# Stick-breaking attention: the suffix sums as split float32r products instead of plain float32 products

## The chip, the core and the metric

The kernel runs on one core of a Trainium2 chip. The metric is the device time of one execution in microseconds (us). The engines are TensorE (PE, matrix products into PSUM), VectorE (DVE), ScalarE (ACT), GpSimd (POOL) and SyncE (SP, which issues the loads). Each works through its own queue in order; they wait for each other on semaphores.

## The reference, cut to what matters

The program is two models one after the other, 256 tokens wide. The change touches the second model's stick-breaking attention (two layers, eight heads of 64):

```python
z = jnp.einsum('bqhd,bkhd->bhqk', q_blk, k).astype(jnp.float32) * scale
past = kpos[None, :] < qpos[:, None]
log_beta = jax.nn.log_sigmoid(z)
log_one_minus = jnp.where(past, jax.nn.log_sigmoid(-z), 0.0)
remain = lax.cumsum(log_one_minus, axis=3, reverse=True) - log_one_minus
w = jnp.where(past, jnp.exp(log_beta + remain), 0.0)
return jnp.einsum('bhqk,bkhd->bqhd', w.astype(v.dtype), v)
```

With s = softplus(z) = max(z, 0) + ln(1 + exp(-|z|)) one has log_one_minus = -s and log_beta = z - s, so the exponent is z minus the sum of s over all keys from the present one on (below the query). That sum over keys is a product with a triangle of ones inside a block of 128 keys, and with a square of ones for the whole later block.

## The kernel before, in words

Weights come in units of 128x1024 float32. Each is loaded by SyncE into `raw` (4 slots), rounded to float32r by ScalarE (`w_hi`, L941), and the remainder `w_lo` = raw - w_hi is formed by VectorE (L1341). A unit is then 24 products of TensorE (L2592 to L2594: high x high, low x high, high x low, for 8 slices), and ScalarE evicts the result (L1230, L1232). ScalarE and VectorE split unit q + 3 while unit q is being multiplied. TensorE starts unit q when the result of unit q - 2 is evicted and `w_lo` of q is there.

The attention stage of a layer of the second model has 48 such units, and the steps of three attentions are laid between them by ticks, one tick to a unit: `block2_items` puts each step on a tick, `ordered` sorts the steps of a tick by `IN_TICK`, and each engine runs its own part of that one list in order. In a tick the unit comes last. The stick-breaking part handles the eight heads as four pairs; tile shapes are 128 keys x (2 heads x 384), the 384 being 256 queries for the first key block and 128 for the second:

- ticks 12 to 15, `sb_scores`: TensorE makes the scores (L2699), VectorE scales and masks them into `sb_z` (L1956), ScalarE makes `sb_e` = |z| and then exp(-|z|) (L1269, L1271);
- ticks 16 and 17, `sb_log`, two pairs each: ScalarE makes ln(1 + e) (L1276), VectorE adds max(z, 0) (L1962). Now `sb_e` holds s, and `sb_soft` is counted up;
- ticks 19 to 22, `sb_remain`: TensorE makes the sums into `turn2`, two banks of PSUM (L2712 to L2714), VectorE subtracts them from `sb_z` (L1968, counts up `sb_diff`), ScalarE takes exp (L1281). As there is one `turn2`, the products of pair j wait for `sb_diff` of pair j - 1;
- ticks 21 to 24, `sb_values` and `sb_out`: the product with the values (L2725) and the split of its result (L1941, L1943).

Beside them stand, at ticks 17, 20 and 24 (and others), rope steps of two tiles: TensorE L2615, VectorE L1860 and one tick later L1867, GpSimd L2141. These are all that GpSimd does in the stage.

A plain float32 product appears in the trace as two instructions, a float32r product as one.

Of the kernel before, what the change touches and what calls it, by code (L numbers as in the profile page):

```python
# [33 lines left out]
F32 = mybir.dt.float32  # L34
F32R = mybir.dt.float32r
ALU = mybir.AluOpType
ACT = mybir.ActivationFunctionType
AX = mybir.AxisListType
P = 128
D = 1024  # L40
KD = D // P
S = 256
# [82 lines left out]
def build_program(nc, x, c, ctx, c_ctx, w_mod, b_mod, norm_g, ffn_w_in, ffn_w_out, w_in, conv_w, pool_w,  # L125
# [3 lines left out]
    K = 1024  # L129
    base = 17 * K  # L130
    region = {}
    at = base
# [6 lines left out]
    def fixed(name, shape, dt, offset):  # L139
        return nc.alloc_sbuf_tensor_at(name, shape, dt, offset=offset)  # L140

    def small(name, shape, dt=F32):
# [55 lines left out]
    sb_z = fixed("sb_z", [P, 4, 2, 384], F32, region["scr"])  # L198
    sb_e = [fixed(f"sb_e{j}", [P, 2, 384], F32, region["scr"] + 12 * K if j == 3 else region["g"] + (30 + 3 * j) * K)
            for j in range(4)]  # L200
    k_swap = fixed("k_swap", [P, S], F32, region["bias"] + 8 * K)
    rope_t = fixed("rope_t", [P, 2, S], F32, region["bias"] + 9 * K)

    const = small("const", [P, CONSTS.shape[1]])
    ones = small("ones", [P, P])
# [40 lines left out]
    for ap in vec_rows:  # L246
        done = 0
        while done < ap.shape[0]:
            n = min(ap.shape[0] - done, P - r % P)
# [12 lines left out]
    def table(name):  # L262
        a, b = CONST_COLS[name]
        return const[:, a:b]

    ident, rot, tri = table("ident"), table("rot"), table("tri")
# [6 lines left out]
    score2, turn2 = psum[:, 4:6, :], psum[:, 6:8, :]  # L273


    def sem(name):
        return nc.alloc_semaphore(name)
# [88 lines left out]
    sb_scores = sem("sb_scores")  # L366
    sb_remain = sem("sb_remain")
    sb_scaled = sem("sb_scaled")
    sb_soft = sem("sb_soft")
    sb_diff = sem("sb_diff")  # L370
    sb_log = sem("sb_log")
    sb_weight = sem("sb_weight")

    c_ready = sem("c_ready")
    mix_pool = sem("mix_pool")
# [223 lines left out]
    def add_job(at, j, start, weights, turn, values):  # L599
# [4 lines left out]
        if j["what"] != "near" or j["qt"] == 1:  # L604
            at(start + values, "out", j)

    IN_TICK = ("values", "sb_values", "weights", "turn", "scores", "sb_scores", "sb_log", "sb_remain", "out", "sb_out",
               "rope_add", "swap", "rope", "turn_v", "bias", "conv_in", "conv_out", "sigmoid", "unit")

    def ordered(ticks):  # L610

        return [item for tick in sorted(ticks) for item in sorted(ticks[tick], key=lambda item: IN_TICK.index(item[0]))]

# [40 lines left out]
    def block2_items(at_):  # L654
        layer = at_["layer"]
        ticks = {}

        def at(tick, what, arg):
            ticks.setdefault(tick, []).append((what, arg))
        for q in range(at_["fill"].n):  # L660
            at(q, "unit", (q, 0, 1))
        for tick, tiles in ((0, (4,)), (1, (0, 1)), (2, (2, 3)), (17, (18, 19)), (20, (22, 23)), (24, (20, 21)), (26, (24, 25))):
            r = dict(tiles=tiles, r=counts["rope"])
            counts["rope"] += 1
            at(tick, "rope", r)
            at(tick + 1, "rope_add", r)
        at(1, "swap", None)
        for tick, j in ((4, 0), (12, 1), (14, 2), (25, 3), (28, 4)):
            at(tick, "turn_v", j)
        jobs = [new_job("swa", pair, 0, layer) for pair in range(4)]  # L670
        for m, j in enumerate(jobs):
            add_job(at, j, SWA_FIRST + 2 * m, 1, 3, 4)
        sb = []
        for pair in range(4):
            z = dict(pair=pair, n=counts["sb"], first=pair == 0)
            counts["sb"] += 1
            sb.append(z)
            at(12 + pair, "sb_scores", z)
            at(16 + pair // 2, "sb_log", z)
            at(19 + pair, "sb_remain", z)  # L680
            at(21 + pair, "sb_values", z)
            at(21 + pair, "sb_out", z)
        moba = [new_job("moba", pair, 0, layer) for pair in range(4)]
        for m, j in enumerate(moba):
            j["first"] = m == 0
            add_job(at, j, 25 + 4 * m, 2, 3, 4)
        for i, tick in enumerate((42, 44, 48)):
            at(tick, "sigmoid", i)
        at_["jobs"], at_["sb"] = jobs + moba, sb
        return ordered(ticks)  # L690
# [241 lines left out]
    def _(act):  # L932
# [14 lines left out]
        for s, name in enumerate(("c", "c_ctx")):  # L947
            ins = act.activation(c_pad[:, :, s], vec(name, 0, KD), ACT.Silu)
# [324 lines left out]
        def act_sb_log(z):  # L1273
            j = z["pair"]
            act.wait_ge(sb_log, z["log0"] + 8 + j)
            act.activation(sb_e[j][:, :, :], sb_e[j][:, :, :], ACT.Ln, bias=ones[:, 0:1]).then_inc(sb_log, 1)  # L1276

        def act_sb_remain(z):
            z_ = sb_z[:, z["pair"], :, :]
            act.wait_ge(sb_diff, z["n"] + 1)  # L1280
            act.activation(z_, z_, ACT.Exp).then_inc(sb_weight, 1)  # L1281
# [6 lines left out]
        def act_attend(at_):  # L1288
            split, turned = set(), set()
            for what, arg in at_["items"]:  # L1290
                if what == "unit":
                    act_unit(at_, *arg, split=arg[0] not in split)
                elif what == "scores":
                    if arg["what"] == "swa":
                        q = SWA_FIRST + 2 * arg["pair"]
                        split_ahead(at_["fill"], q % 4, q // 4)
                        split.add(q)
                    if arg["what"] == "swa" and arg["pair"] > 0:
                        last = at_["jobs"][arg["pair"] - 1]
                        act_turn(last)  # L1300
                        turned.add(last["n"])
                    act_scores(arg)
                elif what == "turn":
                    if arg["n"] not in turned:
                        act_turn(arg)
                elif what == "sb_scores":
                    act_sb_scores(arg)
                elif what == "sb_log":
                    act_sb_log(arg)
                elif what == "sb_remain":  # L1310
                    act_sb_remain(arg)
                elif what == "conv_in":
                    act_conv(at_["mixed"])
                elif what == "pooled":
                    act_pooled(at_["mixed"])
                elif what == "sigmoid":
                    act_sigmoid(at_, arg)
# [713 lines left out]
    def _(pool):  # L2031
# [105 lines left out]
        def pool_rope(r):  # L2137
            w, t0 = len(r["tiles"]), r["tiles"][0]
            cos = table("cos").unsqueeze(1).to_broadcast([P, w, S])
            pool.wait_ge(rope_pe, r["r"] + 1)  # L2140
            pool.tensor_tensor(U2[:, t0:t0 + w, :], U2[:, t0:t0 + w, :], cos, ALU.mult).then_inc(rope_pool, 1)  # L2141

        def pool_norm(nm):
            kind, width = nm["kind"], nm.get("width", S)
            if kind == "first":
                pool.wait_ge(mod_ready, 1)
                pool_w_load(0)
                bias_load(0)
            elif kind in ("plain", "double"):
                for k in range(KD):  # L2150
                    pool.wait_ge(h_hi_done, nm["h0"] + k + 1)
                    pool.tensor_tensor(H2_lo[:, k, :], T2[:, k, :], H2_hi[:, k, :].bitcast(F32), ALU.subtract).then_inc(h_lo_done, 1)

        for kind, ph in plan:
            if kind == "gemm" and ph.kind != "fill":
                pool_gemm(ph)
            elif kind == "norm":
                pool_norm(ph)
            elif kind == "mixers":
                pool_mixers(ph)  # L2160
            elif kind == "attend":
                if ph["block"] == 1:
                    if ph["layer"] + 1 < DEPTH:
                        pool.wait_ge(max_done, ph["jobs"][-1]["n"] + 1)
                        pool.wait_ge(mix_pe, 4)
                        pool_w_load(ph["layer"] + 1)
                        bias_load(ph["layer"] + 1)
                else:
                    for what, arg in ph["items"]:
                        if what == "rope":  # L2170
                            pool_rope(arg)


    @blk.tensor
    def _(pe):
# [525 lines left out]
            ins.then_inc(sb_scores, 1)  # L2701

        def pe_sb_remain(at_, z):
            pe.wait_ge(sb_soft, z["n"] + 1)
            if z["first"]:
                pe.wait_ge(pt_copy, z["free_scores"])
            else:
                pe.wait_ge(sb_diff, z["n"])
            for e in range(2):

                x_ = sb_e[z["pair"]][:, e, :]
                pe.matmul(turn2[:, e, 0:S], tri, x_[:, 0:S], start=True, stop=False)  # L2712
                pe.matmul(turn2[:, e, P:S], ones[:, :], x_[:, S:384], start=False, stop=True)
                ins = pe.matmul(turn2[:, e, S:384], tri, x_[:, S:384], start=True, stop=True)  # L2714
            ins.then_inc(sb_remain, 1)

        def pe_sb_values(at_, z):
# [75 lines left out]
```

## Time and profile before

| | us |
|---|---|
| median of 3 runs (2587.07 to 2588.83) | 2587.65 |
| span of the profiled execution (its own time as the profile has it) | 2584.8 |
| median less span | 2.85 |
| TensorE busy, share of the span | 2541.3, 98% |
| VectorE busy | 1889.3, 73% |
| ScalarE busy | 1137.2, 44% |
| GpSimd busy | 376.0, 15% |

The profile shows one execution, from its first instruction to its last; no other time is listed for that execution. Busy is the time in which an engine had an instruction under way. Products of TensorE overlap each other, so the cost of one is read from the distance between two starts and not from its duration. On the other engines, too, an instruction begins some 0.1 us before the one ahead of it has ended. In a row of the timeline, "x2" are two instructions drawn together, and brackets at the end give the idle time before them and what ended it; no brackets mean no idle time.

### The profile page before, as it was taken

The page shows a single profiled execution, that of the slowest core. Times are in us where ns is not written, and L with a number is a line of the kernel's source. Part 1 is how long each engine was busy: PE and PEld are TensorE (multiplying, and loading weights), DVE is VectorE, ACT ScalarE, POOL GpSimd, SP SyncE. Part 2 cuts the span into 40 slices and gives each one's busy share as a digit, 9 for nine tenths or more (in the row PEclk, how much of TensorE's full clock was granted, in tenths as well). Part 3 has the DMA queues.
Part 4 walks back from the last instruction along what each step waited for, and adds up shares of the span by engine and source line. Part 5 has one row for each costly group of instructions (what it writes and reads, how often), then busy time and mean ns, then how long its engine had stood idle before and what let it go on. Part 6 is the DMA issues. An engine that isn't in the chain of part 4 may idle for free. (4 is left out here: it accounts for less than half of the span.)

```text
span 2584.8 us, 42675 instructions
## 1 busy us (share of the span) xinstructions
PE 2541.3 (98%) x15774; PEld 2238.7 (87%) x15774; DVE 1889.3 (73%) x2915; ACT 1137.2 (44%) x1791; POOL 376.0 (15%) x359
## 2 busy tenths in 40 slices
PE   7999999999999999999999999999999999999999
PEld 4888889779888888888887888889999998999998
DVE  5899985666868678687465777786578877657886
ACT  3222233444222233222244555655656565565655
POOL 2101011141101021000020200210021121002111
PEclk9999999999999999999999999999999999999999
DMA  9566653134454535554232466544566654456664
GB/s 302 169 196 195 196 171 101 58 85 137 150 174 148 175 110 171 159 166 155 88 104 87 123 190 189 159 139 125 161 181 180 186 173 140 122 163 181 179 183 128
DMA packets 653991, 400.48 MB, mean 155 GB/s; under 512 B 12007, under 2 KB 614724, under 8 KB 653698
## 3 DMA queue, kind: packets, MB, share of 16 engines
q1 hardware_dynamic: 651520, 394.67, 50.2%
q0 software_dynamic: 2048, 3.48, 0.9%
q8 instruction: 109, 1.79, 0.3%
q14 instruction: 56, 0.46, 0.1%
q10 hardware_dynamic: 258, 0.09, 0.0%
HBM read 397.14 MB, written 1.05 MB: 154 GB/s over the span
## 5 line engine op out<-in xcount | busy, mean ns | idle before, releaser
L1341 DVE TENSOR_TENSOR w_lo<-raw,w_hi 128x1024 fp32r<-128x1024 f32 x609 | 762.1, 1251 | 262.2 <-ACT w_hi L941 258.5
L941 ACT ACTIVATE w_hi<-raw 128x1024 fp32r<-128x1024 f32 x609 | 639.4, 1053 | 388.4 <-PE psum L2468 180.4
L2466 PE MATMUL psum<-H_both,w_hi 128*128 128x512 f32 x1040 | 405.3, 390 | 0.0
L2468 PE MATMUL psum<-H_both,w_hi 128*128 128x512 f32 x1040 | 405.2, 390 | 0.0
L2467 PE MATMUL psum<-H_both,w_lo 128*128 128x512 f32 x1040 | 405.1, 390 | 0.0
L2092 POOL TENSOR_TENSOR G_both<-g,G_both 128x512 f32 (+3 forms) x132 | 153.5, 1163 | 1343.8 <-ACT G_both L1082 893.7
L1394 DVE SCALAR_TENSOR_TENSOR quad_acc<-quad_ring,c_pad,quad_acc 128x512 f32<-128x512 f32 x448 | 338.2, 813 | 0.8
L2466 PEld LDWEIGHTS psum<-H_both,w_hi 128*128 128x128 f32 x1040 | 195.3, 188 | 40.6 <-DVE H_both L1554 0.3
L2467 PEld LDWEIGHTS psum<-H_both,w_lo 128*128 128x128 f32 x1040 | 195.3, 188 | 40.5
L2468 PEld LDWEIGHTS psum<-H_both,w_hi 128*128 128x128 f32 x1040 | 195.3, 188 | 40.2
L2592 PE MATMUL psum<-H_hi,w_hi 128*128 128x256 f32 x768 | 227.6, 296 | 0.7 <-ACT U L1230 0.7
L2593 PE MATMUL psum<-H_hi,w_lo 128*128 128x256 f32 x768 | 217.4, 283 | 0.0
L2594 PE MATMUL psum<-H_lo,w_hi 128*128 128x256 f32 x768 | 217.3, 283 | 0.0
L2466 PE MATMUL psum<-H_hi,w_hi 128*128 128x256 f32 x720 | 204.7, 284 | 1.8 <-DVE w_lo L1341 1.8
L2467 PE MATMUL psum<-H_hi,w_lo 128*128 128x256 f32 x720 | 204.1, 283 | 0.0
L2468 PE MATMUL psum<-H_lo,w_hi 128*128 128x256 f32 x720 | 204.1, 283 | 0.0
L1082 ACT ACTIVATE G_both<-g 128x512 f32 (+1 forms) x66 | 41.8, 633 | 276.3 <-DVE g L1637 276.3
L2592 PEld LDWEIGHTS psum<-H_hi,w_hi 128*128 128x128 f32 x768 | 147.0, 191 | 10.1 <-issue 9.6
L2466 PE MATMUL psum<-G_both,w_hi 128*128 128x512 f32 (+1 forms) x420 | 154.1, 367 | 1.0 <-DVE w_lo L1341 1.0
L2467 PE MATMUL psum<-G_both,w_lo 128*128 128x512 f32 (+1 forms) x420 | 153.4, 365 | 0.0
L2468 PE MATMUL psum<-G_both,w_hi 128*128 128x512 f32 (+1 forms) x420 | 153.4, 365 | 0.0
L2593 PEld LDWEIGHTS psum<-H_hi,w_lo 128*128 128x128 f32 x768 | 147.2, 192 | 2.9 <-issue 2.9
(309 smaller groups left out, 5550.9 us busy)
## 6 DMA issues: line engine op xcount, KB each, us to landing
raw<-ffn_w_in SPq DMA_DIRECT2D x176, 512.0 KB, 4.6
raw<-w_in SPq DMA_DIRECT2D x148, 512.0 KB, 3.7
quad_ring<-w_mod SPq DMA_DIRECT2D x66, 1024.0 KB, 5.1
raw<-w_up SPq DMA_DIRECT2D x88, 512.0 KB, 4.3
raw<-ffn_w_out SPq DMA_DIRECT2D x64, 512.0 KB, 4.7
raw<-w_out SPq DMA_DIRECT2D x32, 512.0 KB, 4.0
raw<-w_down SPq DMA_DIRECT2D x32, 512.0 KB, 4.3
raw<-ffn_w_out SPq DMA_DIRECT2D x32, 384.0 KB, 3.4
```

What stands on the lines that cost most here:

```text
L941: act.activation(w_hi[:, slot, :], raw[:, slot, :], ACT.Copy).then_inc(hi_done, 1)
L1082: act.activation(G_hi[:, 2 * i + v - 2, 0:width], g32[:, v - 2, 0:width], ACT.Copy).then_inc(g_hi_done, 1)
L1341: dve.tensor_tensor(w_lo[:, slot, :], raw[:, slot, :], w_hi[:, slot, :].bitcast(F32), ALU.subtract).then_inc(lo_done, 1)
L1394: ins = dve.scalar_tensor_tensor(quad_acc[:, s, :], w, c_pad[:, k, s:s + 1], quad_acc[:, s, :], ALU.mult, ALU.add)
L2092: pool.tensor_tensor(lo[:, 2 * i + e, 0:width], g32[:, e, 0:width], hi[:, 2 * i + e, 0:width].bitcast(F32), ALU.subtract).then_inc(g_lo_do ...
L2466: pe.matmul(o, wh, xh[:, k, 0:width], start=k == 0, stop=False)
L2467: pe.matmul(o, wl, xh[:, k, 0:width], start=False, stop=False)
L2468: ins = pe.matmul(o, wh, xl[:, k, 0:width], start=False, stop=k == kk - 1)
L2592: pe.matmul(o, wh, xh[:, k, 0:width], start=k == 0, stop=False)
L2593: pe.matmul(o, wl, xh[:, k, 0:width], start=False, stop=False)
L2594: ins = pe.matmul(o, wh, xl[:, k, 0:width], start=False, stop=k == KD - 1)
```

## The change

The tile of s is split into a float32r high part and a float32r low part, and the triangle and the square of ones are kept in float32r too. ScalarE copies `sb_e` to `sb_high` (`sb_high`, ticks 17 and 18, ahead of `sb_log` in a tick), GpSimd forms `sb_low` = sb_e - sb_high in place (`sb_low`, ticks 18 and 19, after `sb_log`), and once a layer, ahead of its first `sb_low`, copies the triangle and the ones into `tri_r` and `ones_r`. TensorE waits for `sb_low` instead of `sb_soft`, and makes eight float32r products a pair (four a head: triangle by 384 columns of high and of low, square by 128 columns of high and of low) in place of six plain ones (triangle by 256, square by 128, triangle by 128 a head).

```diff
+    sb_low = [fixed(f"sb_low{j}", [P, 2, 384], F32R, region["scr"] + 12 * K if j == 3 else region["g"] + (30 + 3 * j) * K)
+              for j in range(4)]
+    sb_high = fixed("sb_high", [P, 4, 2, 384], F32R, region["x"] + 12 * K)
+    tri_r = fixed("tri_r", [P, P], F32R, region["x"] + 11 * K)
+    ones_r = fixed("ones_r", [P, P], F32R, region["x"] + 11 * K + 512)
...
-    IN_TICK = ("values", "sb_values", "weights", "turn", "scores", "sb_scores", "sb_log", "sb_remain", "out", "sb_out",
+    IN_TICK = ("values", "sb_values", "weights", "turn", "scores", "sb_scores", "sb_high", "sb_log", "sb_low", "sb_remain", "out", "sb_out",
...
             at(16 + pair // 2, "sb_log", z)
+            at(17 + pair // 2, "sb_high", z)
+            at(18 + pair // 2, "sb_low", z)
             at(19 + pair, "sb_remain", z)
...
+        def act_sb_high(z):
+            act.wait_ge(sb_soft, z["n"] + 1)
+            act.activation(sb_high[:, z["pair"], :, :], sb_e[z["pair"]][:, :, :], ACT.Copy).then_inc(sb_high_done, 1)
...
+        def pool_sb_low(z):
+            j = z["pair"]
+            if z["first"]:
+                pool.tensor_copy(tri_r[:, :], tri)
+                pool.tensor_copy(ones_r[:, :], ones[:, :]).then_inc(units_ready, 1)
+            pool.wait_ge(sb_high_done, z["n"] + 1)
+            pool.tensor_tensor(sb_low[j][:, :, :], sb_e[j][:, :, :], sb_high[:, j, :, :].bitcast(F32), ALU.subtract) \
+                .then_inc(sb_low_done, 1)
...
         def pe_sb_remain(at_, z):
-            pe.wait_ge(sb_soft, z["n"] + 1)
+            pe.wait_ge(sb_low_done, z["n"] + 1)
             if z["first"]:
+                pe.wait_ge(units_ready, z["n"] // 4 + 1)
                 pe.wait_ge(pt_copy, z["free_scores"])
             else:
                 pe.wait_ge(sb_diff, z["n"])
             for e in range(2):
-
-                x_ = sb_e[z["pair"]][:, e, :]
-                pe.matmul(turn2[:, e, 0:S], tri, x_[:, 0:S], start=True, stop=False)
-                pe.matmul(turn2[:, e, P:S], ones[:, :], x_[:, S:384], start=False, stop=True)
-                ins = pe.matmul(turn2[:, e, S:384], tri, x_[:, S:384], start=True, stop=True)
+                high, low = sb_high[:, z["pair"], e, :], sb_low[z["pair"]][:, e, :]
+                pe.matmul(turn2[:, e, 0:384], tri_r[:, :], high[:, 0:384], start=True, stop=False)
+                pe.matmul(turn2[:, e, 0:384], tri_r[:, :], low[:, 0:384], start=False, stop=False)
+                pe.matmul(turn2[:, e, P:S], ones_r[:, :], high[:, S:384], start=False, stop=False)
+                ins = pe.matmul(turn2[:, e, P:S], ones_r[:, :], low[:, S:384], start=False, stop=True)
             ins.then_inc(sb_remain, 1)
```

## Rows read from the trace of the kernel before

**Rows 1.** The page, part 1: busy us, share of the span, instructions.

```profile
PE 2541.3 (98%) x15774; PEld 2238.7 (87%) x15774; DVE 1889.3 (73%) x2915; ACT 1137.2 (44%) x1791; POOL 376.0 (15%) x359
```

**Rows 2.** Windows, the attention stages: length, engines' busy us, clock, DMA share, GB/s.

```profile
1736.00:1806.00 70.00, 69.67 (x548) 63.24 (x547) 45.35 (x59) 39.41 (x59) 5.19 (x4) 1.00 0.41 121
2189.00:2259.00 70.00, 69.67 (x549) 63.24 (x548) 45.35 (x59) 39.42 (x59) 5.18 (x4) 1.00 0.42 120
```

**Rows 3.** Timeline of TensorE, pair 0's sums to pair 1's: start, length, instruction.

```profile
1765.06 0.60 PE L2712 MATMUL psum<-sb_e,const 128*128 128x256 f32 x2
1765.49 0.38 PE L2713 MATMUL psum<-sb_e,ones 128*128 128x128 f32 x2
1765.71 0.39 PE L2714 MATMUL psum<-sb_e,const 128*128 128x128 f32 x2
...
1766.73 0.37 PE L2592 MATMUL psum<-H_hi,w_hi 128*128 128x256 f32 x1
1766.93 0.28 PE L2593 MATMUL psum<-H_hi,w_lo 128*128 128x256 f32 x1
1767.05 0.29 PE L2594 MATMUL psum<-H_lo,w_hi 128*128 128x256 f32 x1
...
1769.69 0.60 PE L2712 MATMUL psum<-sb_e,const 128*128 128x256 f32 x2
```

**Rows 4.** Timeline of ScalarE, ticks 15 to 17.

```profile
1755.47 0.85 ACT L1271 ACTIVATE sb_e<-sb_e 128x768 f32<-128x768 f32 x1
1756.22 1.04 ACT L941 ACTIVATE w_hi<-raw 128x1024 fp32r<-128x1024 f32 x1
...
1760.66 1.04 ACT L941 ACTIVATE w_hi<-raw 128x1024 fp32r<-128x1024 f32 x1
1761.61 0.36 ACT L1230 ACTIVATE U<-psum 128x256 f32<-128x256 f32 x1
1761.87 1.90 ACT L1276 ACTIVATE sb_e<-sb_e,ones 128x768 f32<-128x768 f32 x2
```

**Rows 5.** Timeline of VectorE, ticks 16 to 19.

```profile
1759.82 2.17 DVE L1962 SCALAR_TENSOR_TENSOR sb_e<-sb_z,sb_e 128x768 f32<-128x768 f32 x2 [1.30 <-ACT sb_e L1276]
1761.92 1.21 DVE L1341 TENSOR_TENSOR w_lo<-raw,w_hi 128x1024 fp32r<-128x1024 f32 x1
1763.05 1.81 DVE L1962 SCALAR_TENSOR_TENSOR sb_e<-sb_z,sb_e 128x768 f32<-128x768 f32 x2
...
1768.26 0.94 DVE L1968 TENSOR_TENSOR sb_z<-sb_z,psum 128x768 f32<-128x768 f32 x1
```

**Rows 6.** Timeline of TensorE, 512-column float32r products back to back.

```profile
299.98 0.39 PE L2466 MATMUL psum<-G_both,w_hi 128*128 128x512 f32 x1
300.21 0.39 PE L2467 MATMUL psum<-G_both,w_lo 128*128 128x512 f32 x1
```

**Rows 7.** Timeline of GpSimd: 256 and 512 columns of two-input work, not held up.

```profile
1502.61 0.73 POOL L2092 TENSOR_TENSOR G_both<-g,G_both 128x256 f32 x1 [9.24 <-ACT G_both L1072]
...
1759.01 1.30 POOL L2141 TENSOR_TENSOR U<-U,const 128x512 f32<-128x512 f32 x1 [57.76 <-PE psum L2615]
```

**Rows 8.** Timeline of VectorE and GpSimd, one instruction a row (windows 81.3:81.8, 83:84).

```profile
81.21 0.74 DVE L1394 SCALAR_TENSOR_TENSOR quad_acc<-quad_ring,c_pad,quad_acc 128x512 f32<-128x512 f32 x1
...
82.29 1.47 POOL L2092 TENSOR_TENSOR G_both<-g,G_both 128x512 f32 x1 [14.72 <-ACT G_both L1082]
82.53 1.78 DVE L1394 SCALAR_TENSOR_TENSOR quad_acc<-quad_ring,c_pad,quad_acc 128x512 f32<-128x512 f32 x1
```

**Rows 9.** Windows (columns as in rows 2) in and behind stretches short of TensorE work.

```profile
36.60:40.50 3.90, 0.26 (x3) 0.01 (x1) 2.52 (x7) 2.23 (x6) 1.42 (x3) 1.00 1.14 339
41.10:44.40 3.30, 3.30 (x9) 2.54 (x8) 2.50 (x6) 3.30 (x10) 3.30 (x7) 0.50 0.65 77
...
1474.60:1481.50 6.90, 6.09 (x19) 5.26 (x20) 6.57 (x15) 4.32 (x9) 0.00 (x0) 0.51 0.00 0
...
2142.00:2150.00 8.00, 6.14 (x45) 5.44 (x44) 6.24 (x11) 2.39 (x3) 1.61 (x2) 1.00 0.95 276
```

More of the change, by code:

```diff
@@ L372, in build_program @@
     sb_weight = sem("sb_weight")
+    sb_high_done = sem("sb_high_done")
+    sb_low_done = sem("sb_low_done")
+    units_ready = sem("units_ready")
     c_ready = sem("c_ready")
@@ L1309, in act_attend @@
                     act_sb_log(arg)
+                elif what == "sb_high":
+                    act_sb_high(arg)
                 elif what == "sb_remain":
@@ L2171, in _ @@
                             pool_rope(arg)
+                        elif what == "sb_low":
+                            pool_sb_low(arg)
     @blk.tensor
```

## Prediction, made before the kernel was run

> **What bounds the kernel now.** I read the page first, then the two attention stages of the second model, then each engine's order of time in the first of them. TensorE is busy 98% of the span [rows 1] and 99.5% of either attention stage, where VectorE has 65% and ScalarE 56% [rows 2]. The two stages have the same busy times to 0.1 us [rows 2], so I work the first out and double it. Inside it TensorE runs weight units (24 products, 2.9 us) and slips the attention steps between them. What TensorE no longer does is won, and what it newly waits for is lost, one for one.
>
> There is little slack at the place touched. In [rows 3] the first sum product of pair 1 starts at 1769.69. Its code waits for `sb_diff` of pair 0, because `turn2` is one buffer. That subtraction (L1968) starts at 1768.26 and takes 0.94, so it ends at 1769.20 [rows 5], 0.5 us before. The VectorE rows from 1761.92 to there carry no idle time in brackets [rows 5], nor do ScalarE's from 1755.47 to 1761.87 [rows 4]. Both queues are full just where the change adds to them.
>
> **1. The products: a gain of 0.79 us a pair.** Before, a pair is six products in plain float32, seen as twelve instructions. They take from 1765.06 to 1766.73, 1.67 us, and the unit product behind them takes 0.20 to the next (1766.73 to 1766.93) instead of 0.12 (to 1767.05), so 1.75 [rows 3]. After, a pair is eight float32r products, each one instruction: four of 384 columns, four of 128. Float32r of 256 columns goes every 0.12 us [rows 3], of 512 every 0.227 [rows 6] (four in a row begin at 299.98, 300.21, 300.44, 300.66). The line through both is 0.0137 us plus 0.417 ns a column: 0.174 for 384, 0.067 for 128. A pair is 4 x 0.174 + 4 x 0.067 = 0.96 us. No row shows float32r of 128 columns. Lower bound 0.067; upper bound is what a plain product of 128 columns takes, 0.22 (1765.49 to 1765.71, [rows 3]), which makes the pair 1.58 and the gain 0.17. I take 0.067, since the 256 and 512 rows are the same kind of operand, and keep 0.62 a pair for the range.
>
> The Trainium skill, "TensorE: Matmul & The Clock Gate", section "Back-to-back issue gap", gives about 81 ns for a 128-column product with its weight load in a sustained stream; by it the pair would be 0.06 longer. The same sentence gives 131 ns at 512 columns, where this trace has 227 [rows 6], so I don't build on it.
>
> **2. ScalarE: four copies `sb_high`, 128x768.** No row has this copy; the nearest are Abs and Exp of the same shape, 0.75 us from start to start (1755.47 to 1756.22, [rows 4]). Bounds: 0.26 for a 256-wide eviction (1761.61 to 1761.87) and 0.95 for the 1024-wide copy (1760.66 to 1761.61), [rows 4]; I take 0.75. I cost no table load: the copy L941 stands ahead of the third Ln and none is between them [rows 4]. In item order the first two come after unit 16's eviction (1761.61) and ahead of the last two Ln. Ln of pair 2 moves from 1761.87 to 1763.35, 1.5 us. The other two stand before unit 18's w_hi. Behind the copies queue unit 17's eviction, for which unit 19 waits, and w_hi of 20 and 21.
>
> **3. GpSimd: four subtractions `sb_low`, 128x768, and two small copies.** GpSimd takes 0.73 for 256 columns and 1.29 to 1.30 for 512 of two-input work [rows 7], so 1.85 for 768 on that line. Bounds 1.3 (the 512 row) and 2.6 (twice it). The queue has room: 5.2 of 70 us [rows 2]. The two 128-wide copies are at most 0.73 each (the 256-wide row), wait for nothing and stand behind the rope product at 1759.01 [rows 7], so they end by 1761.8, before `sb_high` 0 does.
>
> **4. What the subtractions do to VectorE.** This is the step that decides. [rows 8] shows three things at one place. GpSimd asks at 82.29 while VectorE is inside a row of back-to-back instructions with two SBUF inputs. GpSimd takes 1.47, its 1.29 plus the rest of the instruction in progress. The VectorE instruction next in the queue takes 1.78 instead of 0.74: it stood still while GpSimd ran. So GpSimd gets its turn between two VectorE instructions and costs the second its whole time less about 0.25. L1962, the very instruction of this chain, lost time in the same way: at 1759.82, beside the rope product of [rows 7], two take 2.17, at 1763.05 alone 1.81 [rows 5].
>
> The Trainium skill, "SBUF — State Buffer", section "Who interferes with whom", says a VectorE instruction with two SBUF inputs and a GpSimd instruction that reads SBUF exclude each other for the whole of the one that began first. By the rule each collision costs up to the full 1.85, some 0.2 more than the rows give. That would be 0.7 us more a stage.
>
> Now the queue laid out again, asked-first served first. Exposed on VectorE are L1962 (sb_z, sb_e), w_lo L1341 (raw, w_hi) and rope add L1867; not L1860 and L1968, which read PSUM.
> - `sb_high` 0 runs 1761.85 to 1762.7; `sb_low` 0 then 1762.95 (after w_lo) to 1764.8. L1962 of pair 2 is ready at 1764.3 and begins 1764.6: 0.3 lost.
> - `sb_low` 1 gets in at 1765.4, to 1767.3. L1962 of pair 3, due 1765.5, begins 1767.07: 1.6 lost.
> - rope L1860 free. `sb_low` 2 from 1767.9 to 1769.7; w_lo 20, due 1768.5, begins 1769.5: 1.0 lost.
> - `sb_low` 3 from 1770.6 to 1772.4; L1867, due 1770.65, begins 1772.24: 1.6 lost.
> - w_lo 21 at 1772.8, L1968 of pair 0 at 1774.0, through at 1774.9.
>
> Check: 1.5 from ScalarE plus 0.3 + 1.6 + 1.0 + 1.6 = 6.0, against 1769.2 to 1774.9 = 5.7 (VectorE had a little air at 1768.2).
>
> TensorE: pair 0's product runs at 1764.9 as before (its `sb_low` ends 1764.8), and its 0.79 goes into waiting for unit 17's eviction, now 1766.1 to 1766.5. Unit 19 ends at 1769.4. Pair 1's product starts at 1774.94 instead of 1769.69: 5.25 later, an idle stretch of 5.5. Pairs 1, 2, 3 then give back 3 x 0.79 = 2.4. Later waits are covered: `sb_low` 1 to 3 are through before pair 1 starts, and each next diff has a unit (2.9) to hide in. Sum 5.25 - 2.4 = +2.9 a stage.
>
> **5. The clock.** TensorE idle that long is dear. At 36.6 to 40.5 it has 0.26 us of work, and 41.1 to 44.4 is granted 0.50 (1.2 GHz) [rows 9]. From 1474.6 to 1481.5, behind a norm, it is granted 0.51 [rows 9]. From 2142 to 2150, where a pause of 1.86 us of TensorE lies (6.14 busy of 8), it keeps 1.00 (2.4 GHz) [rows 9]. A bare wait of 5.5 us is longer than the one ahead of 41.1. Price: 3.3 us at half rate, 1.7; bounds 0 and 3.4 (6.9 at half). I take 1.7.
>
> **Sum.** (2.9 + 1.7) x 2 = +9.2 us on the profiled execution's span, 2584.8 to 2594.0. The median of the runs lies 2.85 above that span; I add the same and come to 2596.9, say 2597.
>
> **Rivals.**
> - *The clock holds.* Against it the first case above; for it, that there is one such bare wait in the trace and not a second to confirm it. 2 x 2.9 = 5.8: 2593.5.
> - *GpSimd doesn't hold VectorE up* (it gets only gaps, or L1962 and L1341 pass). Then only the four ScalarE copies remain: w_hi 21 ends 1768.9, w_lo 21 1770.1, L1968 1771.0, pair 1 starts 1.35 late, 1.35 - 2.4 = -1.0 a stage: 2585.6, and 2589.4 with narrow products at 0.22. [rows 8] speaks against it.
> - *All is hidden, the gain comes whole* (the other side). One place: L1968 of pair 0 must end by about 1769.7. It has 0.5 us, and the two early copies put 1.5 ahead of it, unless the copies run far shorter or the loss is caught by idle VectorE time. 8 x 0.79 = 6.3: 2581.3.
> - *Worse.* The same stall with 6.9 us at half clock (3.4) and narrow products at 0.22 (3 x 0.62 = 1.9): 2 x (2.9 + 3.4 + 1.9) = 16.4: 2604.
>
> **Chances.** Forecast 0.42 (2593.5 to 2601, narrow products either way); clock holds 0.15; no hold-up 0.24; all hidden 0.10; worse 0.09. 0.2% (5.2 us) is about what a measurement of this kernel can tell from no change. Forecast, worse and the clock rival are slower: 0.66. The no-hold-up case is the same: 0.24. All hidden is faster: 0.10. The range leaves out the hidden case and the upper half of the worst: 2585 to 2604; the forecast's own is 2593.5 to 2601.
>
> **What would show it.** Step 1: eight product instructions a pair, 0.96 us from first to the next unit. Step 2: the third Ln 1.5 later against its w_hi. Steps 3 and 4: `sb_low` 1.85 or longer, L1962, L1341 and L1867 beside it lengthened by 1 to 1.6. Step 4's end: one wait of TensorE before pair 1's product, 5 us and more, released by L1968. Step 5: granted clock under 1.00 right behind it. I am wrong if that wait is under 2.5 us, or if GpSimd's instructions stretch while VectorE's keep their lengths.

## The result, and the profile after

| | median us (lowest to highest, executions) | profiled execution: own time, span, granted clock |
|---|---|---|
| before | 2587.36 (2586.82 to 2588.83, 4) | its times stand above |
| after | 2600.06 (2599.50 to 2600.43, 4) | 2600.27, 2598.5, 0.993 |

The ratio is 1.0047 (95% interval 1.0036 to 1.0059): 12.7 us slower, where I had forecast 9.2 slower (2597.0). Two things carry nearly all of it: a wait of 5.8 us of TensorE in each attention stage, and a stretch at half the clock that begins near its end.

First part 1 of the page of the kernel after, beside [rows 1].

```profile
PE 2542.5 (98%) x15742; PEld 2238.3 (86%) x15742; DVE 1898.7 (73%) x2915; ACT 1143.4 (44%) x1799; POOL 401.7 (15%) x371
```

TensorE has 32 instructions fewer (8 pairs, 12 to 8 each) and yet 1.2 us more busy time, because some of its work ran at half rate (the windows below). VectorE has the same 2915 instructions and 9.4 us more busy time: none was added, they were lengthened.

The timeline of TensorE in the first attention stage, which answers to [rows 3] (start, length, instruction, idle time ahead of it and its releaser).

```profile
1766.09 0.44 PE L2739 MATMUL psum<-sb_high,tri_r 128*128 128x384 f32 x1
1766.36 0.34 PE L2740 MATMUL psum<-sb_low,tri_r 128*128 128x384 f32 x1
1766.54 0.22 PE L2741 MATMUL psum<-sb_high,ones_r 128*128 128x128 f32 x1
1766.60 0.27 PE L2742 MATMUL psum<-sb_low,ones_r 128*128 128x128 f32 x1
1766.71 0.39 PE L2739 MATMUL psum<-sb_high,tri_r 128*128 128x384 f32 x1
...
1767.60 0.35 PE L2619 MATMUL psum<-H_hi,w_hi 128*128 128x256 f32 x1 [0.16 <-ACT U L1240]
...
1776.52 0.66 PE L2739 MATMUL psum<-sb_high,tri_r 128*128 128x384 f32 x1 [5.81 <-DVE sb_z L1984]
1776.97 0.52 PE L2740 MATMUL psum<-sb_low,tri_r 128*128 128x384 f32 x1
```

Pair 1's first product (L2739 of that unit) has 5.81 us of idle time ahead of it, and its releaser is L1984, the `sb_diff` of pair 0. Before, the place had none [rows 3]. The product of 384 columns is 0.45 us from the next one there, against 0.18 to 0.27 at 1766: it runs at half clock, 1.2 GHz, as the windows below show.

ScalarE, VectorE and GpSimd over the same ticks, which answer to [rows 4, 5, 7] (L1290 is new, L1286 is L1276 of before, L1357 is L1341, L1978 is L1962, L1883 is L1867, L1984 is L1968). In the kernels further down the line numbers shift by a few; go by the tiles.

```profile
1762.88 1.57 ACT L1290 ACTIVATE sb_high<-sb_e 128x768 fp32r<-128x768 f32 x2
1764.35 1.90 ACT L1286 ACTIVATE sb_e<-sb_e,ones 128x768 f32<-128x768 f32 x2
```

```profile
1765.31 4.07 DVE L1978 SCALAR_TENSOR_TENSOR sb_e<-sb_z,sb_e 128x768 f32<-128x768 f32 x2 [0.98 <-ACT sb_e L1286]
1769.30 0.68 DVE L1876 TENSOR_TENSOR rope_t<-psum,const 128x512 f32<-128x512 f32 x1
1769.90 2.26 DVE L1357 TENSOR_TENSOR w_lo<-raw,w_hi 128x1024 fp32r<-128x1024 f32 x1
1772.09 2.28 DVE L1883 TENSOR_TENSOR U<-U,rope_t 128x512 f32<-128x512 f32 x1
...
1775.43 0.94 DVE L1984 TENSOR_TENSOR sb_z<-sb_z,psum 128x768 f32<-128x768 f32 x1
```

```profile
1760.01 1.30 POOL L2157 TENSOR_TENSOR U<-U,const 128x512 f32<-128x512 f32 x1 [57.76 <-PE psum L2642]
...
1762.22 1.02 POOL L2163 CAST ones_r<-ones 128x128 fp32r<-128x128 f32 x1
1763.79 10.03 POOL L2165 TENSOR_TENSOR sb_low<-sb_e,sb_high 128x768 fp32r<-128x768 f32 x4 [0.55 <-ACT sb_high L1290]
```

ScalarE runs the two copies in 1.47 us ahead of the last two Ln. VectorE has no idle time in brackets from 1765.31 to the end of L1984, and three of its rows there, four instructions, are longer than before: L1978 4.07 for two (1.81, [rows 5]), L1357 2.26 (1.21), L1883 2.28 (0.68, in this row of the kernel before):

```profile
1766.52 0.68 DVE L1867 TENSOR_TENSOR U<-U,rope_t 128x512 f32<-128x512 f32 x1
```

GpSimd's four subtractions fill the same stretch, 1763.79 to 1773.8. The row L1876, which reads PSUM, keeps its 0.68.

Three windows around the wait (columns as in [rows 2]).

```profile
1770.50:1775.90 5.40, 0.21 (x2) 0.00 (x1) 5.40 (x4) 2.25 (x3) 3.32 (x2) 1.00 0.33 97
1776.00:1782.80 6.80, 6.28 (x21) 5.28 (x22) 3.78 (x5) 3.85 (x5) 1.28 (x1) 0.50 0.54 157
1782.90:1790.00 7.10, 7.10 (x60) 6.38 (x61) 3.32 (x6) 2.56 (x4) 0.00 (x0) 1.00 0.26 74
```

After 5.4 us with 0.21 us of matmuls the granted clock is 0.50 (1.2 GHz) for 6.8 us, and then 1.00 again. 21 products stand in those 6.8 us, 60 in the 7.1 behind them. The second stage has a stretch at half clock of the same length, but it begins 3.2 us before its wait ends (2236.6), so only half of it falls on work:

```profile
2233.40:2240.20 6.80, 3.65 (x11) 2.97 (x11) 4.95 (x5) 2.06 (x3) 0.46 (x1) 0.50 0.53 152
```

**Where the time went.** The spans differ by 13.7 us. I follow the starts of the same w_lo instruction in both traces. 1.0 is there before either attention stage, in a part that no line of the change touches: 0.7 by 34.3, where TensorE's start waits differ from one execution to the other, and 0.4 more behind the last half-clock stretch of the start, which [rows 9] have at 3.3 us and which lasts 6.8 here. Stage 1 adds 6.97, stage 2 adds 5.78, and nothing is added behind.

- Pair 1's product starts 5.82 later than before (1776.52 - 1.01 - 1769.69).
- Pairs 1 to 3 give back 0.60 each (worked out under the products alone), 1.8. That leaves 4.0 a stage.
- The clock: half of the 6.28 us of work that fell on it in stage 1, 3.1; half of 3.65 in stage 2, 1.8.

4.0 + 3.1 = 7.1 and 4.0 + 1.8 = 5.8, against 6.97 and 5.78. Nothing of size is left over.

### The profile page after: what moved, and what is told of

Same layout as the page of the kernel before. It is cut to its first block and busy times, and to the rows that moved or that the text cites. A ratio compares the mean times of both kernels' runs of the same rounds, so it can differ in the third digit from the quotient of the medians.

```text
span 2598.5 us, 42631 instructions
## 1 busy us (share of the span) xinstructions
PE 2542.5 (98%) x15742; PEld 2238.3 (86%) x15742; DVE 1898.7 (73%) x2915; ACT 1143.4 (44%) x1799; POOL 401.7 (15%) x371
## 5 line engine op out<-in xcount | busy, mean ns | idle before, releaser
L1357 DVE TENSOR_TENSOR w_lo<-raw,w_hi 128x1024 fp32r<-128x1024 f32 x609 | 763.2, 1253 | 261.8 <-ACT w_hi L951 258.1
```

The source lines that it names most:

```text
L1357: dve.tensor_tensor(w_lo[:, slot, :], raw[:, slot, :], w_hi[:, slot, :].bitcast(F32), ALU.subtract).then_inc(lo_done, 1)
```

## The experiments

All times are medians; the ratio is against the kernel before on the same chip (2587.89 beside products alone, and the copies, products and subtractions, and subtraction on VectorE; 2587.90 beside memsets and high part, a tick later; 2587.98 beside the rest). "A stage" is how much later than in the kernel before the same w_lo comes at the end of an attention stage, less what it was late at its start, from the profiled execution. VectorE makes w_lo some units ahead of TensorE, so a wait of TensorE in the last units isn't in that number yet; it matters in two rows, marked with a star.

| kernel | median us | ratio (95%) | a stage, us | idle ahead of pair 1's product | half clock in the stage |
|---|---|---|---|---|---|
| products alone | 2583.90 | 0.9985 (0.9976 to 0.9994) | -1.91, -1.93 | 0.30 | none |
| and the copies | 2588.35 | 1.0001 (0.9992 to 1.0010) | -0.31, -0.31 | 1.43 | none |
| products and subtractions | 2598.50 | 1.0041 (1.0027 to 1.0055) | +4.71, +5.32 | 4.79 | 6.8 us each |
| memsets for subtractions | 2585.10 | 0.9989 (0.9980 to 0.9998) | -1.92, -1.93 | 0.28 | none |
| all, the wait filled | 2596.63 | 1.0033 (1.0021 to 1.0045) | +4.11, +4.11 | 1.03 | none |
| all, old products | 2603.49 | 1.0060 (1.0047 to 1.0074) | +7.67, +7.68 | 5.53 | 6.8 us each |
| subtraction on VectorE | 2596.36 | 1.0035 (1.0022 to 1.0047) | +4.19, +4.25 | 3.66, ahead of pair 0 | 6.8 us each |
| all, other ticks | 2586.74 | 0.9995 (0.9986 to 1.0004) | -2.18, -2.20 * | none (0.64 ahead of pair 0's next unit) | none |
| high part alone | 2582.33 | 0.9975 (0.9964 to 0.9985) | -3.65, -3.64 | 0.86 | none |
| high part, a tick later | 2581.10 | 0.9971 (0.9961 to 0.9980) | -5.22, -5.22 * | none | none |

The stars: measured on TensorE's own units at the end of the stage, the gain is less, -0.97 and -0.96 for other ticks, -4.00 and -3.98 for the high part a tick later.

### Products alone, and with the copies

The first has VectorE write the sum s in float32r, and takes it for both halves; no copy, no subtraction. The second keeps ScalarE's copy and takes the high part twice; no subtraction. In both the low part is left out and the high part counts twice.

```
# products alone (L1978, in the product loop)
-  dve.scalar_tensor_tensor(sb_e[j][:, :, :], ...)
+  dve.scalar_tensor_tensor(sb_low[j][:, :, :], ...)        # float32r
-  pe.wait_ge(sb_low_done, z["n"] + 1)
+  pe.wait_ge(sb_soft, z["n"] + 1)
-  high, low = sb_high[:, z["pair"], e, :], sb_low[z["pair"]][:, e, :]
+  high, low = sb_low[z["pair"]][:, e, :], sb_low[z["pair"]][:, e, :]
# with the copies
-  pe.wait_ge(sb_low_done, z["n"] + 1)
+  pe.wait_ge(sb_high_done, z["n"] + 1)
+  high, low = sb_high[:, z["pair"], e, :], sb_high[:, z["pair"], e, :]
```

> The eight float32r products a pair are kept; ScalarE's copies and GpSimd's subtractions are left out. VectorE's L1978 writes the sum s rounded to float32r, and both products of a pair of products read that tile, so the low part is left out and the high part counted twice. Theory (the products alone are a gain, all of the loss comes from what feeds them): no wait of TensorE over 1 us in the stage, clock 1.00 there, 2.8 us less a stage, about 2581.8 (8 x 0.79 = 6.3 at most, 2581). Rival (the loss is in the products or the wider accumulation in PSUM): at or above 2587.

> As the changed kernel, with ScalarE's four copies a stage but without GpSimd's subtractions: the products read the high part twice (low part left out). Theory: only ScalarE's 1.5 us before the third Ln is left of the delay; pair 1's product starts 1.2 to 1.6 us later than before, TensorE waits 1.7 there, clock holds at 1.00, -0.8 to -1.0 a stage, about 2585.5. Rival (the copies in ScalarE's full queue are the main cause): a wait of 4 us or more and a time above 2592.

Measured: 2583.90 and 2588.35. Both are slower than expected (2581.8 and 2585.5), and the first rival, at or above 2587 for the products alone, is out. The pair of products in the first kernel, on TensorE's timeline (the first product, the narrow ones, and the unit product behind them):

```profile
1766.71 0.34 PE L2735 MATMUL psum<-sb_low,tri_r 128*128 128x384 f32 x1
1766.89 0.34 PE L2736 MATMUL psum<-sb_low,tri_r 128*128 128x384 f32 x1
1767.06 0.22 PE L2737 MATMUL psum<-sb_low,ones_r 128*128 128x128 f32 x1
1767.12 0.27 PE L2738 MATMUL psum<-sb_low,ones_r 128*128 128x128 f32 x1
1767.23 0.39 PE L2735 MATMUL psum<-sb_low,tri_r 128*128 128x384 f32 x1
...
1767.81 0.34 PE L2615 MATMUL psum<-H_hi,w_hi 128*128 128x256 f32 x1
```

From 1766.71 to 1767.81 a pair takes 1.10 us, not 0.96. The second 384-column product of the pair of heads, which follows a 128-column one, starts 0.23 before its successor instead of 0.174, and the narrow ones take 0.06 and 0.11. The unit product behind takes 0.17 to the next one, 0.05 more than its 0.12. With that, as the 1.75 of before was counted, a pair is 1.15 and the gain 0.60; charged to the narrow products alone they cost 0.11 each. Four pairs would give 2.4 a stage; 1.9 arrives. The difference is lost ahead of pair 1, whose product starts 0.58 behind the one before it instead of 0.12 (idle time 0.30 in the row's brackets).

The copies cost 1.6 a stage (-0.31 against -1.91). Of that 1.13 is the wait ahead of pair 1, 1.43 instead of 0.30. Nearly all of the rest is the unit behind pair 0, which starts 0.43 later: it waits for unit 17's eviction, and ScalarE has that behind the copies.

```profile
1768.20 0.36 PE L2616 MATMUL psum<-H_hi,w_hi 128*128 128x256 f32 x1 [0.28 <-ACT U L1240]
1772.74 0.41 PE L2736 MATMUL psum<-sb_high,tri_r 128*128 128x384 f32 x1 [1.43 <-DVE sb_z L1984]
```

### Products and subtractions, no copies

VectorE writes s in float32r as in the products alone, and GpSimd subtracts that tile from itself, once `sb_soft` is there; same shape, two SBUF inputs, no ScalarE copy. The low part is left out (it is zero).

```
-  pool.wait_ge(sb_high_done, z["n"] + 1)
-  pool.tensor_tensor(sb_low[j], sb_e[j], sb_high[:, j], ALU.subtract)
+  pool.wait_ge(sb_soft, z["n"] + 1)
+  pool.tensor_tensor(sb_high[:, j], sb_low[j], sb_low[j], ALU.subtract)
```

> The reverse of the one before: GpSimd's four subtractions of the same size (two float32 inputs in SBUF, float32r out) directly behind L1978, without ScalarE's copies. L1978 writes float32r and GpSimd subtracts that tile from itself, so the low part is zero. Theory (GpSimd holds VectorE up): L1978, L1357 and L1883 beside a subtraction last 1.5 us longer, TensorE waits 5 us or more before pair 1's product, the clock falls to 1.2 GHz behind it, the time is that of the changed kernel within 3 us, 2597 to 2601. Rival (the chain of steps is only longer, GpSimd doesn't disturb): the wait is under 1 us, since the subtractions have the units to hide in, and the time is that of the products alone, 2582.

Measured: 2598.50, as expected, with the wait at 4.79 (5 or more expected). VectorE and then GpSimd of this kernel:

```profile
1765.15 4.36 DVE L1977 SCALAR_TENSOR_TENSOR sb_low<-sb_z,sb_e 128x768 fp32r<-128x768 f32 x2
1769.43 0.68 DVE L1875 TENSOR_TENSOR rope_t<-psum,const 128x512 f32<-128x512 f32 x1
1770.04 1.88 DVE L1356 TENSOR_TENSOR w_lo<-raw,w_hi 128x1024 fp32r<-128x1024 f32 x1
1771.84 1.95 DVE L1882 TENSOR_TENSOR U<-U,rope_t 128x512 f32<-128x512 f32 x1
```

```profile
1764.12 9.12 POOL L2164 TENSOR_TENSOR sb_high<-sb_low 128x768 fp32r<-128x768 f32 x4
```

The two L1978 lose 2.5 us together, L1357 0.7 and L1883 1.3. So most of the wait comes without ScalarE's copies. The two causes add: 0.30 + 1.13 (copies) + 4.49 (subtractions) = 5.92, against 5.81 in the whole change.

### Memsets in place of the subtractions

Is it GpSimd being busy that stretches VectorE, or what GpSimd reads? This kernel is the one just shown, but GpSimd writes `sb_high` in three memsets a pair and reads nothing, at the same place in its queue (semaphores between the memsets aren't shown).

```
+  pool.wait_ge(sb_soft, z["n"] + 1)
+  pool.memset(sb_high[:, j, 0:1, :], 0.0)
+  pool.memset(sb_high[:, j, :, :], 0.0)
+  pool.memset(sb_high[:, j, :, :], 0.0)
```

> As the run with the subtractions alone, but GpSimd fills the second tile with zeros in three memsets (384, 768 and 768 columns, about 1.9 us together) in place of one subtraction of 1.86: it is busy as long, in the same place, and TensorE waits for it as before, but it reads nothing. The low part is zero in both. Theory (GpSimd and VectorE exclude each other where both read SBUF, VectorE with two inputs): L1978, L1357 and L1883 keep their alone lengths (0.95, 1.22, 0.68), pair 1's wait is 0.3 to 0.6 us as in the products alone, clock 1.00, 1.9 us less a stage, about 2584. Rival (any work of GpSimd beside VectorE slows it, or the chain's length costs): a wait of 4 us or more, half clock, 2598.

Measured: 2585.10 (about 2584 expected), 13.4 us less than with subtractions. VectorE, then GpSimd:

```profile
1765.53 1.81 DVE L1978 SCALAR_TENSOR_TENSOR sb_low<-sb_z,sb_e 128x768 fp32r<-128x768 f32 x2
1767.27 0.68 DVE L1876 TENSOR_TENSOR rope_t<-psum,const 128x512 f32<-128x512 f32 x1
1767.87 1.21 DVE L1357 TENSOR_TENSOR w_lo<-raw,w_hi 128x1024 fp32r<-128x1024 f32 x1
```

```profile
1766.43 0.42 POOL L2165 MEMSET sb_high<- 128x384 f32 x1
1766.91 0.74 POOL L2167 MEMSET sb_high<- 128x768 f32 x1
1767.71 0.75 POOL L2169 MEMSET sb_high<- 128x768 f32 x1
```

GpSimd is at work for 1.9 of the 2.0 us from 1766.43 to 1768.46, beside VectorE's L1978 and L1357, and these keep the lengths that they have alone, 1.81 for two and 1.21. The wait is 0.28. GpSimd being busy and writing costs nothing here; the subtraction with its two SBUF inputs does. A GpSimd instruction of this size with one SBUF input wasn't tried. The small casts of the change read one (128 columns), and VectorE's L1978 and L1357 beside them are 0.1 longer each:

```profile
1763.01 1.31 DVE L1357 TENSOR_TENSOR w_lo<-raw,w_hi 128x1024 fp32r<-128x1024 f32 x1
```

That is the w_lo of the whole change beside the cast at 1762.22; alone it takes 1.21.

The Trainium skill, "SBUF — State Buffer", section "Who interferes with whom", says of such a pair: a VectorE instruction with two SBUF inputs contends with a GpSimd one that reads SBUF, not with one that only writes it. The rows of the last two kernels agree.

### The wait filled: what the clock costs

Nothing is changed but that TensorE runs 40 products of 256 columns (S is 256; they take 4.96 us) into a PSUM buffer that it overwrites later, ahead of the waits of pair 1. VectorE and GpSimd are as late as in the whole change.

```
+  if z["pair"] == 1:
+      at_least(pe, o_done, z["out_first"])
+      for _ in range(40):
+          pe.matmul(OUT[:, 0:S], ones_r[:, :], sb_high[:, 0, 0, 0:S], start=True, stop=True)
```

> The whole change, and ahead of pair 1's wait TensorE makes 40 products of 256 columns into a free bank that nobody reads (4.8 us of the 5.8 us it would stand idle). Theory (the stand-still itself lets the clock fall, and that costs on top): the granted clock stays 1.00 through both stages, pair 1's product starts where it did in the changed kernel (the wait for L1984 is as late as ever), and the time is 4 to 5.5 us below the changed kernel, 2594.5 to 2596. Rival (the lower clock has another cause, or costs nothing): clock 0.5 behind the wait as before and 2600.

Measured: 2596.63, a little above the 2594.5 to 2596 expected; in the profiled execution +4.11 in both stages. The product of pair 1, and a window over the stage:

```profile
1775.38 0.41 PE L2744 MATMUL psum<-sb_high,tri_r 128*128 128x384 f32 x1 [1.03 <-DVE sb_z L1985]
```

```profile
1747.00:1785.00 38.00, 36.45 (x286) 34.07 (x285) 26.81 (x24) 24.95 (x34) 15.05 (x8) 1.00 0.38 108
```

The clock stays at 1.00 over all 38 us. With the same lateness of L1984 the stages cost 4.1 instead of 6.97 and 5.78, so the half clock cost 2.9 and 1.7, 4.5 in all; from the windows of the whole change I had read 3.1 and 1.8. The medians are 3.4 apart, and 4.05 if each is taken against the kernel before beside it (12.7 and 8.65 slower). The 4.1 itself stands beside the 4.0 that lateness less gain gives.

### The old products behind the same split

The split is kept, ScalarE's copy, GpSimd's subtraction and all, but the subtraction writes over `sb_high`, so that s stays in `sb_e`; TensorE takes the old plain products on `sb_e`.

```
-  pool.tensor_tensor(sb_low[j], sb_e[j], sb_high[:, j], ALU.subtract)
+  pool.tensor_tensor(sb_high[:, j], sb_e[j], sb_high[:, j], ALU.subtract)
-  pe.matmul(turn2[:, e, 0:384], tri_r[:, :], high[:, 0:384], ...)   # and three more
+  pe.matmul(turn2[:, e, 0:S], tri, x_[:, 0:S], ...)
+  pe.matmul(turn2[:, e, P:S], ones[:, :], x_[:, S:384], ...)
+  pe.matmul(turn2[:, e, S:384], tri, x_[:, S:384], ...)
```

> Copies and subtractions as in the change (the difference goes to the place of the high part, so that s stays), TensorE waits for them, but the products are the plain float32 ones of before on s; what the copies and subtractions make is not used. Theory: the wait before pair 1 is 5.2 to 5.8 us as in the changed kernel, half clock behind it, and the products' gain is missing: 2 to 4 us above the changed kernel, 2602 to 2604. Rival (the float32r products cost as much as they save there): 2600 within 1.

Measured: 2603.49, as expected, 3.4 above the whole change, and 2.8 if each is taken against the kernel before beside it. So the products' gain is worth some 3 us where it is taken behind the wait, near the 6 x 0.60 = 3.6 of pairs 1 to 3 in two stages. The stages are only 2.6 apart, since in the first the half clock falls on less work here (3.60 us of it, against 6.28).

### The subtraction on VectorE

```
+  def dve_sb_low(z):
+      dve.wait_ge(sb_high_done, z["n"] + 1)
+      dve.tensor_tensor(sb_low[j], sb_e[j], sb_high[:, j], ALU.subtract)
```

> The whole change with the subtraction on VectorE in place of GpSimd, same ticks. VectorE pays about 0.87 us for each instead of losing 0.3 to 1.6. Theory: the queue relaid gives 2.2 us more a stage without the clock (pair 0's product 3.9 late, pair 1's another 1.4), so 2591.8, and up to 2596 if the clock falls behind the first wait; below the changed kernel in either case by 4 us or more. Rival (it is the length of the chain that costs, whoever subtracts): 2600 again.

Measured: 2596.36, 3.7 less than with GpSimd, just above the 2591.8 to 2596 expected. VectorE's two subtractions (the first two pairs), and TensorE's largest wait in the stage (engine, line, releaser: us in total, times, longest):

```profile
1768.12 1.82 DVE L1984 TENSOR_TENSOR sb_low<-sb_e,sb_high 128x768 fp32r<-128x768 f32 x2
```

```profile
PE psum L2744 <- DVE sb_low L1984: 3.7, 1, 3.7
```

A subtraction takes VectorE 0.9 us, and stretches nothing; on GpSimd it takes 1.85 and cost VectorE 0.6 to 1.7. But in its tick it stands behind the last L1978, a rope product and a w_lo, so now pair 0 itself waits, 3.66 us, and the clock falls there too (half from 1768.4 on, 0.7 before the wait ends). Moving the work to VectorE is no cure at this place.

### All of the change, in other ticks

Three things are changed at once: all of ScalarE's copies go behind the last Ln (copy 0 by the order inside a tick), the subtractions are spread, and the remaining steps of a pair move to the next tick, so that pair 1's sums stand a unit later.

```
- IN_TICK = (..., "sb_high", "sb_log", "sb_low", ...)
+ IN_TICK = (..., "sb_log", "sb_high", "sb_low", ...)
- at(17 + pair // 2, "sb_high", z)
- at(18 + pair // 2, "sb_low", z)
- at(19 + pair, "sb_remain", z)
+ at((17, 20, 20, 20)[pair], "sb_high", z)
+ at((18, 20, 21, 22)[pair], "sb_low", z)
+ at(20 + pair, "sb_remain", z)      # values and out: 22 + pair for 21 + pair
```

> The whole change with other ticks: the high copies at 17, 20, 20, 20 and after the logarithms of their tick, the low subtractions at 18, 20, 21, 22, the sums and all behind them one tick later (20 to 23 and 22 to 25). Theory (where GpSimd's subtractions meet VectorE's full stretch decides, not their amount): relaid queue without a wait of TensorE over 1.5 us, clock 1.00, 1.7 us less a stage, 2584.5, at least 12 us below the changed kernel. Rival (the same four subtractions a stage cost VectorE the same wherever they are, and TensorE with it): within 4 us of 2600.

Measured: 2586.74 (2584.5 expected), 13.3 less than the change as made. VectorE, then GpSimd:

```profile
1763.53 1.81 DVE L1978 SCALAR_TENSOR_TENSOR sb_e<-sb_z,sb_e 128x768 f32<-128x768 f32 x2
...
1765.87 2.26 DVE L1357 TENSOR_TENSOR w_lo<-raw,w_hi 128x1024 fp32r<-128x1024 f32 x1
```

```profile
1764.89 2.16 POOL L2165 TENSOR_TENSOR sb_low<-sb_e,sb_high 128x768 fp32r<-128x768 f32 x1 [2.36 <-ACT sb_high L1290]
1770.51 2.21 POOL L2165 TENSOR_TENSOR sb_low<-sb_e,sb_high 128x768 fp32r<-128x768 f32 x1 [3.46 <-ACT sb_high L1290]
...
1773.92 1.85 POOL L2165 TENSOR_TENSOR sb_low<-sb_e,sb_high 128x768 fp32r<-128x768 f32 x1
```

The collisions aren't gone (the w_lo at 1765.87 still takes 2.26), but ahead of the first diff there is one instead of four, and the later ones fall where VectorE has air. The third subtraction, at 1773.92, meets nothing at first and takes 1.85. Each stage is 2.2 faster; 1.2 of that is given back a little later, in the same way as in the last kernel below. Against the kernel before it is no difference that the runs can tell (0.9986 to 1.0004). What each of the three moves is worth was not taken apart.

### The high part alone, and a tick later

With one float32r product for two (the low part is left out), and no copy or subtraction, VectorE writing s in float32r as in the products alone; the second kernel also moves the remaining steps to the next tick.

```
-  pe.matmul(turn2[:, e, 0:384], tri_r[:, :], low[:, 0:384], start=False, stop=False)
-  ins = pe.matmul(turn2[:, e, P:S], ones_r[:, :], low[:, S:384], start=False, stop=True)
```

> Only the high part: L1978 writes s rounded to float32r, two float32r products a head (384 and 128 columns), no copies, no subtractions; the low part is left out. Theory: a pair takes 0.55 instead of 1.75, pair 1's product waits 0.8 to 1.0 for L1984, 4.0 us less a stage, 2580, and no lower clock. Rival (VectorE's queue, not TensorE, sets the stage once products are short): no more than the 1.9 us a stage of the eight products alone, 2584.

> The high part alone (low part left out) with the sums and all behind them one tick later. Theory (the 0.9 us that TensorE still waited for L1984 is a matter of the tick): no wait over 0.4 us, 4.6 us less a stage, 1 to 2 us under the high part alone, 2579 to 2581. Rival (VectorE and ScalarE have no slack a tick later either): 2582.

Measured: 2582.33 and 2581.10, both faster than the kernel before, by 0.25% and 0.29%, without the low part of the sums. 2580, and 2579 to 2581, were expected. The stages of the second are 1.6 better than those of the first, and 1.2 of this is given back in the last units of the stage, where TensorE has one new wait (engine, line, releaser: us in total, times, longest):

```profile
PE psum L2638 <- DVE vt L1868: 0.8, 1, 0.8
```

So even a split that cost nothing would have little to win here. At the old ticks it is the products alone, 4.0 us of 2588; with the low part left out too it is 5.7, and 6.8 a tick later.

## Why the prediction came out as it did

The sign, the place and the mechanism were those of the forecast. Its 2597 was 3.1 us short of the 2600.06, which lies inside the range and inside the forecast's own. By its steps:

- **Step 1 (products).** A pair takes 1.15 (with what the unit product behind it loses) instead of 0.96, the gain is 0.60 instead of 0.79. The failing term is the 128-column product, taken from the line through 256 and 512 columns at 0.067 and measured at 0.11. The wider ones were right. Over the six pairs that count this is 1.1 us. The Trainium skill, "TensorE: Matmul & The Clock Gate", section "Back-to-back issue gap", has about 81 ns there, nearer than my line: the forecast for this width would have been better with it.
- **Step 2 (copies).** Right: the third Ln came 1.47 later against its w_hi (1.5 forecast). The two kernels of the first test show its share of the wait, 1.1, and 1.6 of the lateness of pair 1.
- **Step 3 (GpSimd).** The subtraction was right, 1.85 where it meets nothing. The two small copies were bounded at 0.73 and take 1.02 each, so the second (at 1762.22) ends at 1763.24, which is 1762.2 with the 1.0 of the start taken off, instead of 1761.8. That is before `sb_high` 0 is through at 1763.7, so the subtractions don't wait for it; the two copies stretched L1978 and a w_lo by 0.1 each.
- **Step 4 (GpSimd against VectorE).** Right in place and nearly in size: the losses are 0.6, 1.66, 1.04 and 1.60, together 4.9, where I had 0.3, 1.6, 1.0 and 1.6, together 4.5. The wait is 5.81 against 5.5, released by L1984. The lateness, 5.82, was mis-sized by 0.57, 0.3 of it in the first collision. The rival that GpSimd doesn't hold VectorE up falls with the two kernels of subtractions and memsets. The losses are 0.4 above the rows' estimate, between it and the 0.7 more a stage that I had put beside it by the Trainium skill, "SBUF — State Buffer", section "Who interferes with whom". That section calls the shared port pair an exclusive lock; for how long, "for the whole instruction", it says only beside VectorE's two-port modes. Here a collision cost 0.6 to 1.7 of the 1.85.
- **Step 4's end.** Pair 0's gain was indeed lost, and pairs 1 to 3 give 1.8 and not 2.4. Stage without clock: +4.0 against +2.9, and +4.1 where the wait was filled. This is the largest part of the miss, 2 x 1.1.
- **Step 5 (clock).** It fell, in both stages. I took 3.3 us at half rate and kept 6.9 as a bound; it was 6.8, the bound. It cost 3.1 and 1.8 by the windows, 2.9 and 1.7 by the kernel with the wait filled, not 1.7 twice; in stage 2 only half of it fell on work. With the wait filled the clock stays up: that it is this wait that drops it is shown, and so the rival that the clock holds falls. The row that spoke for that rival, the clock kept behind a pause of 1.86 us, is weaker than I took it: in the products alone the same pause is followed by half clock.

```profile
2144.41 0.67 PE L2638 MATMUL psum<-U,const 128*128 128x256 f32 x2 [1.85 <-DVE U L1607]
2145.20:2148.60 3.40, 3.40 (x18) 3.40 (x18) 2.69 (x5) 0.00 (x0) 0.69 (x1) 0.50 0.95 280
```

- **What lies around.** I had 2.85 above the span, from the median of before; this execution has 1.8, and 1.0 of its span was lost at the start. The two nearly cancel, which is luck.

The other rivals: "all is hidden" needed L1968 to end by 1769.7, and it ended near 1775.4 when the 1.0 of the start is taken off. "Worse" had the full half clock right (6.8) and the narrow products wrong (0.11, not 0.22).

Left open: why a half-clock stretch outside the attention stages is there in one execution and not in another. At the start the last one is 3.4 us long in some and 6.8 or more in others. The pause of 1.85 us ahead of the rope products stands twice in each of the twelve traces, near 1692 and 2145, and in 10 of these 24 places 3.4 us of half clock follow. What remains of the wait when GpSimd reads one input from PSUM wasn't tried.

## What to carry to other kernels

Work put on an idle GpSimd isn't free if it reads two operands from SBUF while VectorE does the same: count each collision at up to nearly GpSimd's whole time on VectorE's queue (0.6 to 1.7 of 1.85 us here), and then ask who waits for VectorE; other ticks, for the split and for what follows it, were worth 13 us here, more than the edit could win. Where TensorE is 98% busy, price a new wait of some 5 us at its length and, as here, 2 to 3 us more for the clock behind it. And if a step is slow because of where it stands, try its place before its operation.

## What the runs showed that I had not expected

- GpSimd's 128x128 CAST to float32r takes 1.02 us, more than its 0.73 for a two-input instruction of 256 columns [rows 7].
- GpSimd's memsets (0.42 us for 384 columns, 0.74 for 768) don't stretch VectorE's two-input instructions beside them, and the 128-column CASTs stretch them by 0.1 each.
- A 128-column float32r product makes the step from the next wide one to its successor 0.05 us longer (0.23 for 0.174), so its price lies partly in its neighbour's row.
- The half-clock stretches at the long waits of the attention stages (3.66 to 5.81 us) were all 6.8 us long; at the waits of 1.43 us there was none, at the pauses of 1.85 us near 1692 and 2145 there was none in 14 places and 3.4 us in 10.
